# Two-layer attention and expert step on one core: the probabilities and reciprocals turned by pairs of 64-row transposes instead of whole 128-row ones

## The chip, the cores and the metric

The kernel runs on one core of one Trainium2 chip. The metric is the device time of one execution in microseconds; of several executions the median counts.

## The reference, cut to what matters

One inference step of a two-layer model with D = 1024 and 16 heads, all in float32. The 640 tokens are 512 latent tokens and 128 context tokens. Layer 0 mixes tokens by latent attention (MLA), layer 1 by neighbourhood attention (NAT); each is followed by a mixture of 16 experts.

```python
# layer 0, for each head: 64 + 32 columns of q and k, 64 of v
s = einsum('bqhd,bkhd->bhqk', q_blk, k).astype(float32) * MLA_SCALE
p = softmax(s, axis=-1)
o = einsum('bhqk,bkhd->bqhd', p, v)          # context tokens read 128 keys, latent tokens 640
x = x + gate * (o.reshape(B, S, 1024) @ w_o)
# layer 1, for each head: a clamped window of local keys with a bias, and the 128 cached keys
p = softmax(concat([s_loc * NAT_SCALE + bias, s_ctx * NAT_SCALE]), axis=-1)
o = einsum('brnqhd,brankhd->brnqhd', p_loc, vg) + einsum('bhrnqc,bchd->brnqhd', p_ctx, v_ctx)
```

## The kernel before

The kernel is written with semaphores by hand: each engine (PE = TensorE, ACT = ScalarE, DVE = VectorE, POOL, SP) has its own instruction list, and waits on counts that others raise. The order on each engine is therefore fixed in the program. PSUM is one tensor `PS` of 8 banks with 512 float32 columns each.

Both attentions run 40 units of work `w` (`NW`), in eight pairs of heads (`p`), with five query tiles of 128 tokens for each pair (`i`); `ORDER` puts the context tile first (`i == 0`), then the four latent tiles. Inside a unit `par` is 0 or 1 for the two heads of the pair. A unit passes through these steps, each one iteration of the loop later than the one before where the stages allow it:

- Scores on PE (`mla_scores`, lines 979 and 980 for latent tiles, 982 for the context tile; `nat_scores`, lines 1242, 1247 and 1249). MLA has 640 key columns for each head, in banks 0 and 1 for the first head and 2 and 3 for the second; the context tile has 128. NAT has 384 or 128.
- Row maximum on DVE (line 1844 in MLA, 2199 and 2203 in NAT), then the exponential on ACT (line 1481), which also sums each row. The exponentials P lie in `Pm` (MLA) or `Pn` (NAT), tokens on the partitions.
- P is turned, so that keys lie on the partitions, by PE transposes of 128x128 blocks against an identity (line 723, called by `mla_pT` and `nat_pT`). They go to banks 4 and 5, and in MLA the fifth block of each head to bank 6. ACT copies the first head's blocks out (`pT_out`, line 1489) and DVE the second head's (line 1821), in MLA 512 and 768 columns, in NAT 384 and 384.
- The values product on PE (`mla_pv`, line 1010; `nat_pv`, line 1275), 64 output partitions for each head, into bank 7.
- The division by the row sums: DVE takes the reciprocals of the two sums (`rinv`, line 1813), and PE spreads them over a tile of 64 partitions for each head by two float32 products with the identity (`rinv_rows`, line 1020), into bank 6. ACT copies the values product out of PSUM (`o_out`, line 1496), and DVE multiplies it by the spread rows (`o_out` of DVE, a multiply on line 1621).

In MLA, iteration `w` of PE first waits until both copies (`pT_out`) of unit w-2 are through (`a_pa`, `a_pd`). Then it may turn q for a coming head (`q_head`, also line 723; at i = 0 and i = 3), run a slice of the modulation product (`ada`, line 738; at i = 1), or build keys (`k_heads`, line 938; at i = 2). Then it runs the scores of w, the reciprocal rows of w-2, the transposes of w-1 and the values product of w-2. At i = 0 the reciprocal rows also wait for ACT's copy of the turned q (`q_out`, line 1411). ACT's order in an iteration is `q_out` or `k_half` if any, exponentials of w (two), `pT_out` of w-1, `o_out` of w-2. DVE's order is maxima of w (two), `pT_out` of w-1, `o_out` of w-2, `rinv` of w.

In NAT, iteration `w` of PE runs scores of w, transposes of w-2, reciprocal rows and values product of w-3. ACT runs the exponentials of w, `pT_out` of w-2, `o_out` of w-3. DVE runs maxima of w, `rinv` of w-1 (which waits for the values product of w-3), `pT_out` of w-2, `o_out` of w-3 (which waits for ACT's `o_out`).

Of the kernel before, what the change touches and what calls it, by code (L numbers as in the profile page):

```python
# [29 lines left out]
P = 128  # L30
# [86 lines left out]
def build(nc, a, o):  # L117

    with ExitStack() as ctx:
# [45 lines left out]

        def big(off, n, k=None):
            assert off + n <= 20480
            v = BIG[:, off:off + n]
            return v if k is None else v.rearrange("p (k n) -> p k n", k=k)
# [129 lines left out]
        RB = 6 * 512 + 256  # L299
# [417 lines left out]
        def _(pe):  # L717
# [246 lines left out]
            def mla_scores(w):  # L964
# [6 lines left out]
                for par in range(2):  # L971
# [12 lines left out]

            def mla_pT(w):

                if w >= 1:
                    pe.wait_ge(a_pa, w)
                    pe.wait_ge(a_pd, w)
                blocks = NT if w % NT else 1  # L990
                for par in range(2):
                    pe.wait_ge(a_ex, 2 * w + par + 1)
                    for c in range(blocks):
                        dst = bank(4 + par, P, c * P) if c < 4 else bank(6, P, par * P)
                        ins = transpose(dst, Pm[w % 2][par][:, c * P:(c + 1) * P])
                    ins.then_inc(a_pt, 1)

            def mla_pv(w):
# [5 lines left out]
                cols = slice(t * P, (t + 1) * P) if i else slice(0, P)  # L1004
                blocks = [(c, c) for c in range(NT)] if i else [(0, 5)]
                for c, kt in blocks:
                    for par in range(2):
                        h = 2 * p + par
                        at = 1024 + par * P if c == 4 else par * 512 + c * P
                        ins = pe.matmul(PS[64 * par:64 * par + 64, 7 * 512 + cols.start:7 * 512 + cols.stop],  # L1010
# [3 lines left out]

            def rinv_rows(l, w):

                at = 108 + 2 * (w % 2)
                pe.wait_ge(a_ri, NW * l + w + 1)
                for par in range(2):
                    pe.matmul(PS[64 * par:64 * par + 64, RB:RB + P], st[:, at + par:at + par + 1].to_broadcast([P, 64]), ident,  # L1020
                              start=True, stop=True)

            for w in range(NW + 2):
# [28 lines left out]
                if w >= 2:  # L1052
                    pe.wait_ge(a_pd, w - 1)
                    pe.wait_ge(a_o, w - 2)
                    rinv_rows(0, w - 2)
                if 1 <= w <= NW:
                    mla_pT(w - 1)
                if w >= 2:
                    mla_pv(w - 2)
# [192 lines left out]
            def nat_pT(w):  # L1252
# [3 lines left out]
                for par in range(2):  # L1256
                    pe.wait_ge(a_ex, 2 * NW + 2 * w + par + 1)
                    for c in range(3 if w % NT else 1):
                        ins = transpose(bank(4 + par, P, c * P), Pn[w % 3][par][:, c * P:(c + 1) * P])
                    ins.then_inc(a_pt, 1)  # L1260

            def nat_pv(w):
# [4 lines left out]
                pe.wait_ge(a_o, NW + w)  # L1267
                rinv_rows(1, w)
                cols = slice(t * P, (t + 1) * P) if i else slice(0, P)
                vals = [[nv[:, 0], nv[:, 1], nvc], [nvs[:, 0], nvs[:, 1], nvc], [nvs[:, 1], nvs[:, 2], nvc],  # L1270
                        [nv[:, 2], nv[:, 3], nvc], [nv[:, 4]]][t]
                for c, v in enumerate(vals):
                    for par in range(2):
                        h = 2 * p + par
                        ins = pe.matmul(PS[64 * par:64 * par + 64, 7 * 512 + cols.start:7 * 512 + cols.stop],
# [10 lines left out]
            for w in range(NW + 3):  # L1286
# [6 lines left out]
                if w >= 3:  # L1293
                    nat_pv(w - 3)
# [5 lines left out]
        def _(act):  # L1300
# [182 lines left out]
            def pT_out(l, w, dst, n):  # L1483

                g = NW * l + w
                act.wait_ge(a_pt, 2 * g + 1)
                if w >= 2:
                    act.wait_ge(a_pv, g - 1)
                act.activation(dst[:, 0:n], bank(4, n), ACT.Copy).then_inc(a_pa, 1)

            def o_out(l, w):
# [4 lines left out]
                act.activation(OT[:, p, t * P:(t + 1) * P], bank(7, P, t * P if i else 0), ACT.Copy).then_inc(a_oc, 1)  # L1496
# [4 lines left out]
            for w in range(NW + 2):  # L1501
# [14 lines left out]
                if 1 <= w <= NW:  # L1516
                    pT_out(0, w - 1, PTm[(w - 1) % 2], 512 if (w - 1) % NT else P)
# [73 lines left out]
            for w in range(NW + 3):  # L1591
# [10 lines left out]
                if 2 <= w < NW + 2:  # L1602
                    pT_out(1, w - 2, PTn[w % 2][0], 384 if (w - 2) % NT else P)
# [8 lines left out]
        def _(dve):  # L1612
# [193 lines left out]
            def rinv(l, w):  # L1806
# [6 lines left out]
                dve.reciprocal(st[:, 108 + at:110 + at], st[:, 104 + at:106 + at]).then_inc(a_ri, 1)  # L1813
# [9 lines left out]
            def o_out(l, w):  # L1823
# [5 lines left out]
                tt(ot, ot, PS[:, RB:RB + P], ALU.mult).then_inc(a_o, 1)  # L1829

            for w in range(NW + 2):
# [13 lines left out]
                if 1 <= w <= NW:  # L1845
                    n = 768 if (w - 1) % NT else P
                    pT_out(0, w - 1, PTm[(w - 1) % 2][:, 512:512 + n], PS[:, 5 * 512:5 * 512 + n])
# [333 lines left out]
            for w in range(NW + 3):  # L2181
# [24 lines left out]
                if 2 <= w < NW + 2:  # L2206
                    n = 384 if (w - 2) % NT else P
                    pT_out(1, w - 2, PTn[w % 2][1][:, 0:n], bank(5, n))
# [65 lines left out]
```

## Time and profile before

| what | value |
|---|---|
| median of 3 runs | 1399.61 us (1393.13 to 1405.5) |
| profiled execution, span from first to last instruction | 1404.2 us |
| mean granted TensorE clock, share of full | 0.978 |
| MLA attention, 161.0 to 395.5 us of the span | PE busy 220.27 of 234.50 us |
| NAT attention, 968.5 to 1072.0 us of the span | PE busy 95.37 of 103.50 us |
| whole span | PE 91%, DVE 40%, ACT 24%, POOL 17% |

The span is one profiled execution; it lies inside the range of the three runs. A PE instruction's duration runs from its start to the modelled end of its results, so instructions that follow each other overlap in the record, and PE can be called busy in a stretch in which its array is not full. "PEld" is the loading of the stationary operand.

### The profile page before, as it was taken

How to read it: one execution, taken by the hardware profiler on the slowest of the kernel's cores; microseconds unless marked ns; L12 is line 12 of the kernel's file. 1: busy time of each engine (PE TensorE's matmuls, PEld its weight loads, DVE VectorE, ACT ScalarE, POOL GpSimd, SP SyncE). 2: the span in 40 equal slices, each digit the busy share in tenths (PEclk: the TensorE clock that was granted, in tenths of full speed). 3: DMA queues.
4: the chain of work that ended last, by engine and by line, in shares of the span. 5: the costliest groups of instructions: out<-in, count | busy, mean ns of one | idle time of the engine just before them, and what ended most of it. 6: DMA issues, size and time to landing. Idle time of an engine off the chain costs nothing.

```text
span 1404.2 us, 19127 instructions
## 1 busy us (share of the span) xinstructions
PE 1283.3 (91%) x7399; PEld 740.6 (53%) x7399; DVE 568.4 (40%) x1454; ACT 339.7 (24%) x823; POOL 232.8 (17%) x298
## 2 busy tenths in 40 slices
PE   5999899999999989998949999999998998999991
PEld 3665466666654554444424455656775446445440
DVE  5122344444535664444322000002664576444443
ACT  3121344444422310000012000003664231000102
POOL 7122300010010012123221100013221001211231
PEclk8999999999999999999979999999999999999996
DMA  9413211122464459999583363145122615999966
GB/s 388 148 39 153 87 62 62 62 105 78 179 247 164 152 193 390 381 380 395 118 249 125 121 225 120 61 173 165 50 66 95 242 62 225 391 379 380 337 171 210
DMA packets 45449, 267.82 MB, mean 191 GB/s; under 512 B 6980, under 2 KB 13460, under 8 KB 31520
## 3 DMA queue, kind: packets, MB, share of 16 engines
q1 hardware_dynamic: 22672, 192.85, 35.1%
q0 software_dynamic: 16928, 52.77, 13.8%
q10 hardware_dynamic: 5760, 20.97, 3.8%
q8 instruction: 60, 0.98, 0.3%
q14 instruction: 29, 0.24, 0.0%
HBM read 230.19 MB, written 34.81 MB: 189 GB/s over the span
## 4 chain that ended last, share of the span: by engine, by line
PE 70%; DMA 14%; DVE 6%; issue 5%; ACT 4%; DVEq 0%; ACTq 0%; POOLq 0%; SPq 0%
PE PS L851 12%; DMA xrows<-big,info 10%; PE PS L1217 10%; PE PS L1079 10%; PE PS L1127 9%; PE PS L723 8%; PE PS L1144 4%; PE PS L979 4%; PE PS L738 3%; DMA xrows<-big 3%; PE PS L1010 2%; PE PS L938 2%; PE PS L1020 2%; DVE big L1621 1%; ACT weights L1481 1%
## 5 line engine op out<-in xcount | busy, mean ns | idle before, releaser
L1079 PE MATMUL PS<-weights,ht 128*128 128x512 f32 x320 | 142.3, 596 | 2.3 <-DVE ht L1621 1.6
L1217 PE MATMUL PS<-ht,weights 128*128 128x128 f32 (+1 forms) x512 | 140.2, 434 | 1.5 <-PE PS L738 0.9
L723 PE MATMUL PS<-const,big 128*128 128x128 f32 (+2 forms) x611 | 90.1, 284 | 37.8 <-DVE big L2151 17.8
L851 PE MATMUL PS<-weights,ht 128*128 128x336 f32 (+1 forms) x320 | 118.2, 528 | 2.6 <-ACT ht L1399 1.6
L1127 PE MATMUL PS<-big 128*128 128x512 f32 x256 | 115.8, 606 | 4.7 <-DVE big L2068 4.7
L723 PEld LDWEIGHTS PS<-const,big 128*128 128x128 f32 (+2 forms) x611 | 74.1, 144 | 84.1 <-issue 58.2
L1217 PEld LDWEIGHTS PS<-ht,weights 128*128 128x128 f32 x512 | 77.8, 191 | 64.1 <-issue 64.1
L1079 PEld LDWEIGHTS PS<-weights,ht 128*128 128x128 f32 x320 | 59.0, 190 | 69.7 <-issue 69.7
L1530 ACT ACTIVATE big<-PS 128x256 f32<-128x256 f32 x34 | 13.1, 385 | 329.4 <-PE PS L1127 329.4
L851 PEld LDWEIGHTS PS<-weights,ht 128*128 128x128 f32 x320 | 61.0, 193 | 54.5 <-issue 41.1
L1127 PE MATMUL PS<-weights,big 128*128 128x512 f32 x192 | 84.4, 592 | 0.0
L663 POOL DMA_INDIRECT xrows<-big,info x28 | 47.0, 1678 | 221.5 <-DMA xrows<-big,info 213.8
L541 POOL DMA_DIRECT2D modrows<-modrow x32 | 18.7, 586 | 389.0 <-DVE modrow L1621 271.6
L1127 PEld LDWEIGHTS PS<-big 128*128 128x128 f32 x256 | 48.5, 194 | 60.8 <-issue 58.9
L1621 DVE TENSOR_TENSOR big<-PS,big 128x512 f32<-128x512 f32 (+1 forms) x70 | 44.2, 672 | 88.4 <-PE PS L1144 46.7
L1481 ACT ACTIVATE rows<-PS,stats 128x640 f32<-128x640 f32 (+1 forms) x80 | 56.6, 708 | 77.6 <-DVE stats L1844 69.1
L1844 DVE TENSOR_REDUCE stats<-PS 128x1 f32<-128x640 f32 (+1 forms) x80 | 56.8, 718 | 39.6 <-PE PS L980 37.8
L979 PE MATMUL PS<-big 96*128 96x512 f32 x128 | 67.8, 611 | 3.0 <-PE PS L738 1.3
L1144 PE MATMUL PS<-rows,big 128*128 128x512 f32 x144 | 65.0, 594 | 1.0 <-DVE big L2082 1.0
L851 PE MATMUL PS<-weights,rows 128*128 128x384 f32 (+1 forms) x168 | 61.0, 519 | 0.8 <-PE PS L851 0.6
L1621 DVE TENSOR_TENSOR big<-big,PS 128x256 f32<-128x256 f32 x34 | 14.3, 420 | 109.1 <-ACT big L1530 109.1
L1144 PE MATMUL PS<-weights,big 128*128 128x512 f32 x128 | 57.6, 593 | 0.0
(247 smaller groups left out, 1815.3 us busy)
## 6 DMA issues: line engine op xcount, KB each, us to landing
weights<-in_ada SPq DMA_DIRECT2D x22, 2048.0 KB, 8.8
big<-in_gu SPq DMA_DIRECT2D x16, 2048.0 KB, 19.9
weights<-in_gu SPq DMA_DIRECT2D x12, 2048.0 KB, 21.1
rows<-in_down SPq DMA_DIRECT2D x18, 1024.0 KB, 12.4
weights<-in_down SPq DMA_DIRECT2D x16, 1024.0 KB, 16.0
ht<-in_gu SPq DMA_DIRECT2D x6, 2048.0 KB, 22.3
weights<-in_qkv SPq DMA_DIRECT2D x6, 2048.0 KB, 10.2
weights<-in_wo SPq DMA_DIRECT2D x4, 2048.0 KB, 8.6
```

Source lines behind the costliest of these rows:

```text
L663: pool.indirect_dma_start(xD[l], bass.IndirectOffsetOnAxis(ap=token.bitcast(U32), axis=0), yb[par], None, compute_op=ALU.add).then_inc(e_y ...
L723: return pe.transpose(dst, src, const[0:n, C_ID:C_ID + n])
L738: ins = pe.matmul(PS[32 * g:32 * g + 2, ada_out_at(i):ada_out_at(i) + P], condT[:, 2 * k:2 * k + 2], w[:, k, g * P:(g + 1) * P], start=(k ...
L851: ins = pe.matmul(bank(4 + u % 2, n), lhs(k), rhs(k), start=(k == 0), stop=(k == ks - 1))
L979: pe.matmul(bank(2 * par), lhs, kTh[h % 4][0:QD, 0:512], start=True, stop=True)
L1079: ins = pe.matmul(bank(4 + j), OT[:, k, t * P:(t + 1) * P], w[j][:, k, :], start=(k == 0), stop=(k == KD - 1))
L1127: ins = pe.matmul(bank(0), gatT[:, k, :], w[:, k, :], start=(k == 0), stop=(k == KD - 1))
L1144: ins = pe.matmul(bank(out + n), actT[:, k, :], w[:, k, n * 512:(n + 1) * 512], start=(k == 0), stop=(k == 1))
L1217: ins = pe.matmul(bank(bb, n1 - n0), w[:, k, m * P:(m + 1) * P], hT[:, k, n0:n1], start=(k == 0), stop=(k == KD - 1))
L1481: act.activation(dst, src, ACT.Exp, scale=sign, bias=st[:, 100 + at:101 + at], accum_out=st[:, 104 + at:105 + at]).then_inc(a_ex, 1)
L1621: return dve.tensor_tensor(dst, x, y, op)
L1844: dve.tensor_reduce(st[:, at:at + 1], bank(2 * par, n), AXX, ALU.max, negate=True).then_inc(a_mx, 1)
```

## The change

Every 128-row transpose of P becomes two transposes of 64 rows each: the lower 64 partitions of the block against the lower 64 columns of the identity, the upper against the upper. Each half writes 64 columns over all 128 partitions, and the two halves go to two PSUM banks, 512 columns apart. In MLA the first head's blocks take banks 4 and 5 and the second head's banks 6 and 7, at 64 columns for each block; in NAT both heads use banks 4 and 5. The copies put the halves together again: in MLA ACT takes the first head's 640 columns and DVE the second head's 640; in NAT ACT takes bank 4 and DVE bank 5, both heads each, and ACT waits until both heads are turned.

The reciprocal rows are no longer a product: DVE writes each reciprocal into 64 columns of an SBUF tile (`spread_rinv`, 128 columns for a unit), and PE turns this tile with one pair of half transposes into banks 6 and 7 at column 320. In MLA it stands between the two heads' transposes, in NAT behind them.

The values product moves out of bank 7 in MLA, into bank 1 at column 256, a bank that also holds columns 512 to 639 of the first head's scores. So `mla_pv` of w-2 waits for the first exponential of w, and the second score product of the first head waits for `o_out` of w-3. In NAT it stays in bank 7.

```diff
+        spread_rinv = [R[:, 1280:1536], R[:, 4608:4864]]
...
-        RB = 6 * 512 + 256
+        RI = 6 * 512 + 320
+        PV = (512 + 256, 7 * 512)
...
+        def mla_blocks(w, par):
+
+            n = NT if w % NT else 1
+            dst = PTm[w % 2][:, par * 640:par * 640 + n * P].rearrange("p (c r n) -> p c r n", r=2, n=64)
+            src = PS[:, (4 + 2 * par) * 512:(6 + 2 * par) * 512].rearrange("p (r c n) -> p c r n", r=2, n=64)
+            return dst, src[:, 0:n]
+
+        def nat_blocks(w, r):
+
+            n = 3 if w % NT else 1
+            at = 6400 + w % 2 * 768
+            dst = W[:, at:at + 768].rearrange("p (x c r n) -> p x c r n", x=2, r=2, n=64)[:, :, 0:n, r]
+            src = bank(4 + r).rearrange("p (x c n) -> p x c n", x=2, n=64)
+            return dst, src[:, :, 0:n]
...
+            def transpose_halves(dst, src, at):
+
+                for r in range(2):
+                    rows = slice(64 * r, 64 * r + 64)
+                    ins = pe.transpose(dst[:, at + 512 * r:at + 512 * r + 64], src[rows], const[rows, C_ID + 64 * r:C_ID + 64 * r + 64])
+                return ins
...
                     if t < CTX:
                         pe.matmul(bank(2 * par), lhs, kTh[h % 4][0:QD, 0:512], start=True, stop=True)
+                        if par == 0 and w >= 3:
+                            pe.wait_ge(a_oc, w - 2)
...
+            def rinv_rows(l, w):
+
+                at = w % 2 * P
+                pe.wait_ge(a_ri, NW * l + w + 1)
+                pe.wait_ge(a_o, NW * l + w)
+                transpose_halves(PS, spread_rinv[l][:, at:at + P], RI)
+
             def mla_pT(w):
 
-                if w >= 1:
-                    pe.wait_ge(a_pa, w)
-                    pe.wait_ge(a_pd, w)
                 blocks = NT if w % NT else 1
                 for par in range(2):
+                    if w >= 1:
+                        pe.wait_ge((a_pa, a_pd)[par], w)
+                    if par and w >= 1:
+                        rinv_rows(0, w - 1)
                     pe.wait_ge(a_ex, 2 * w + par + 1)
                     for c in range(blocks):
-                        dst = bank(4 + par, P, c * P) if c < 4 else bank(6, P, par * P)
-                        ins = transpose(dst, Pm[w % 2][par][:, c * P:(c + 1) * P])
+                        ins = transpose_halves(PS, Pm[w % 2][par][:, c * P:(c + 1) * P], (4 + 2 * par) * 512 + c * 64)
                     ins.then_inc(a_pt, 1)
 
             def mla_pv(w):
...
-                cols = slice(t * P, (t + 1) * P) if i else slice(0, P)
+                if w + 2 < NW:
+                    pe.wait_ge(a_ex, 2 * (w + 2) + 1)
...
-            def rinv_rows(l, w):
-
-                at = 108 + 2 * (w % 2)
-                pe.wait_ge(a_ri, NW * l + w + 1)
-                for par in range(2):
-                    pe.matmul(PS[64 * par:64 * par + 64, RB:RB + P], st[:, at + par:at + par + 1].to_broadcast([P, 64]), ident,
-                              start=True, stop=True)
...
-                        ins = transpose(bank(4 + par, P, c * P), Pn[w % 3][par][:, c * P:(c + 1) * P])
+                        ins = transpose_halves(PS, Pn[w % 3][par][:, c * P:(c + 1) * P], 4 * 512 + par * 256 + c * 64)
...
-                dve.reciprocal(st[:, 108 + at:110 + at], st[:, 104 + at:106 + at]).then_inc(a_ri, 1)
+                dst = spread_rinv[l][:, w % 2 * P:(w % 2 + 1) * P].rearrange("p (x n) -> p x n", x=2)
+                dve.reciprocal(dst, st[:, 104 + at:106 + at].unsqueeze(2).to_broadcast([P, 2, 64])).then_inc(a_ri, 1)
```

## Rows read from the trace of the kernel before

**Rows 1.** Busy time by stretch: MLA, NAT, and one inside the first experts.

```profile
161.00:395.50 234.50, 220.27 (x2080) 149.22 (x2078) 112.06 (x215) 105.02 (x259) 18.50 (x32) 1.00 0.24 91
968.50:1072.00 103.50, 95.37 (x1034) 74.72 (x1034) 66.31 (x260) 68.45 (x237) 17.00 (x24) 1.00 0.24 68
...
560.00:595.00 35.00, 35.00 (x105) 17.00 (x104) 15.84 (x30) 2.95 (x6) 5.11 (x4) 1.00 1.02 379
```

**Rows 2.** Timeline, MLA, latent tile i = 4: start, duration, engine, line.

```profile
298.94 1.12 PE L979 MATMUL PS<-big 96*128 96x512 f32 x2
...
301.30 0.44 PE L1020 MATMUL PS<-const,stats 128*64 128x128 f32 x4
...
301.67 1.07 PEld L723 LDWEIGHTS PS<-const,rows 128*128 128x128 f32 x10 [0.17 <-issue]
...
301.93 0.19 ACT L1481 ACTIVATION_READ_ACCUMULATOR rows<-PS,stats 128x1 f32 x1
302.32 0.80 ACT L1481 ACTIVATE rows<-PS,stats 128x640 f32<-128x640 f32 x1 [0.20 <-issue]
302.91 1.07 PEld L1010 LDWEIGHTS PS<-rows,big 128*64 128x64 f32 x20 [0.17 <-issue]
...
303.10 0.59 ACT L1489 ACTIVATE route<-PS 128x512 f32<-128x512 f32 x1
304.15 0.50 PEld L723 LDWEIGHTS PS<-const,big 128*96 128x96 f32 x5 [0.17 <-issue]
```

**Rows 3.** Timeline, MLA, the context tile i = 0 that follows.

```profile
305.69 0.44 PE L1020 MATMUL PS<-const,stats 128*64 128x128 f32 x4 [0.34 <-ACT big L1411]
...
308.55 1.64 PEld L738 LDWEIGHTS PS<-weights,condT 128*2 128x2 f32 x64 [0.17 <-issue]
```

**Rows 4.** Timeline, MLA, i = 1 and the start and end of i = 2.

```profile
285.04 0.27 ACT L1489 ACTIVATE rows<-PS 128x128 f32<-128x128 f32 x1
...
285.36 0.20 PEld L938 LDWEIGHTS PS<-rows,weights 128*64 128x64 f32 x4 [0.31 <-ACT rows L1489]
...
288.09 0.30 PEld L979 LDWEIGHTS PS<-big 96*128 96x128 f32 x2 [0.39 <-issue]
...
293.24 0.50 PEld L723 LDWEIGHTS PS<-const,big 128*96 128x96 f32 x5 [0.98 <-ACT route L1489]
```

**Rows 5.** Timeline: four products of 128 columns, whole array, and in two 64-row tiles.

```profile
304.74 0.61 PE L982 MATMUL PS<-big 96*128 96x128 f32 x4
...
1006.74 0.39 PE L1247 MATMUL PS<-big 64*128 64x128 f32 x4
```

**Rows 6.** Groups of instructions by shape: count, busy us, mean ns, idle before.

```profile
L723 PEld LDWEIGHTS PS<-const,rows 128*128 128x128 f32 x338 | 36.3, 140 | 7.0 <-issue 6.9
...
L723 PEld LDWEIGHTS PS<-const,big 128*96 128x96 f32 x80 | 8.1, 126 | 10.1 <-ACT route L1489 3.9 <-issue 3.2 <-ACT rows L1489 3.0
...
L1585 ACT ACTIVATE big<-PS 128x640 f32<-128x640 f32 x8 | 5.6, 704 | 135.1 <-PE PS L1217 135.1
```

**Rows 7.** Timeline, NAT, from i = 4 to the context tile and beyond.

```profile
1012.97 0.62 ACT L1481 ACTIVATE weights<-weights,stats 128x384 f32<-128x384 f32 x1 [0.83 <-DVE stats L2199]
...
1015.64 0.61 ACT L1481 ACTIVATE weights<-weights,stats 128x384 f32<-128x384 f32 x1 [0.83 <-DVE stats L2199]
...
1016.86 0.47 ACT L1489 ACTIVATE weights<-PS 128x384 f32<-128x384 f32 x1
...
1017.55 0.64 PEld L723 LDWEIGHTS PS<-const,weights 128*128 128x128 f32 x6 [0.61 <-ACT weights L1489]
...
1018.10 0.37 ACT L1481 ACTIVATE weights<-PS,stats 128x128 f32<-128x128 f32 x1 [0.61 <-issue]
...
1019.50 0.28 ACT L1496 ACTIVATE ht<-PS 128x128 f32<-128x128 f32 x1 [0.22 <-PE PS L1275]
1019.57 0.17 DVE L1813 RECIPROCAL stats<-stats 128x2 f32<-128x2 f32 x1 [1.36 <-PE PS L1275]
...
1020.94 0.62 ACT L1481 ACTIVATE weights<-weights,stats 128x384 f32<-128x384 f32 x1 [1.16 <-DVE stats L2199]
```

More of the change, by code:

```diff
@@ L1008, in mla_pv @@
                         h = 2 * p + par
-                        at = 1024 + par * P if c == 4 else par * 512 + c * P
-                        ins = pe.matmul(PS[64 * par:64 * par + 64, 7 * 512 + cols.start:7 * 512 + cols.stop],
+                        at = par * 640 + c * P
+                        ins = pe.matmul(PS[64 * par:64 * par + 64, PV[0]:PV[0] + P],
                                         mv[:, kt, h * VD:(h + 1) * VD], PTm[w % 2][:, at:at + P],
@@ L1051, in _ @@
                         pe.wait_ge(q_ea, 2 * p + 4)
[L1052 to L1055, printed above, removed]
                 if 1 <= w <= NW:
@@ L1058, in _ @@
                 if w >= 2:
+                    if w > NW:
+                        pe.wait_ge(a_pd, NW)
+                        rinv_rows(0, w - 2)
                     mla_pv(w - 2)
@@ L1274, in nat_pv @@
                         h = 2 * p + par
-                        ins = pe.matmul(PS[64 * par:64 * par + 64, 7 * 512 + cols.start:7 * 512 + cols.stop],
+                        ins = pe.matmul(PS[64 * par:64 * par + 64, PV[1]:PV[1] + P],
                                         v[:, h * VD:(h + 1) * VD], PTn[w % 2][par][:, c * P:(c + 1) * P],
@@ L1293, in _ @@
                 if w >= 3:
+                    rinv_rows(1, w - 3)
                     nat_pv(w - 3)
@@ L1481, in exp, with pT_out @@
                 act.activation(dst, src, ACT.Exp, scale=sign, bias=st[:, 100 + at:101 + at], accum_out=st[:, 104 + at:105 + at]).then_inc(a_ex, 1)
-            def pT_out(l, w, dst, n):
+            def pT_out(l, w, dst, src):
                 g = NW * l + w
-                act.wait_ge(a_pt, 2 * g + 1)
+                act.wait_ge(a_pt, 2 * g + 1 + l)
                 if w >= 2:
                     act.wait_ge(a_pv, g - 1)
-                act.activation(dst[:, 0:n], bank(4, n), ACT.Copy).then_inc(a_pa, 1)
+                act.activation(dst, src, ACT.Copy).then_inc(a_pa, 1)
             def o_out(l, w):
@@ L1495, in o_out @@
                 act.wait_ge(a_pv, NW * l + w + 1)
-                act.activation(OT[:, p, t * P:(t + 1) * P], bank(7, P, t * P if i else 0), ACT.Copy).then_inc(a_oc, 1)
+                act.activation(OT[:, p, t * P:(t + 1) * P], PS[:, PV[l]:PV[l] + P], ACT.Copy).then_inc(a_oc, 1)
             warm(ACT.Exp)
@@ L1516, in _ @@
                 if 1 <= w <= NW:
-                    pT_out(0, w - 1, PTm[(w - 1) % 2], 512 if (w - 1) % NT else P)
+                    pT_out(0, w - 1, *mla_blocks(w - 1, 0))
                 if w >= 2:
@@ L1602, in _ @@
                 if 2 <= w < NW + 2:
-                    pT_out(1, w - 2, PTn[w % 2][0], 384 if (w - 2) % NT else P)
+                    pT_out(1, w - 2, *nat_blocks(w - 2, 0))
                 if w >= 3:
@@ L1828, in o_out @@
                 ot = OT[:, p, t * P:(t + 1) * P]
-                tt(ot, ot, PS[:, RB:RB + P], ALU.mult).then_inc(a_o, 1)
+                rows = PS[:, 6 * 512:8 * 512].rearrange("p (r n) -> p r n", r=2)[:, :, RI - 6 * 512:RI - 6 * 512 + 64]
+                ot = ot.rearrange("p (r n) -> p r n", r=2)
+                tt(ot, ot, rows, ALU.mult).then_inc(a_o, 1)
             for w in range(NW + 2):
@@ L1845, in _ @@
                 if 1 <= w <= NW:
-                    n = 768 if (w - 1) % NT else P
-                    pT_out(0, w - 1, PTm[(w - 1) % 2][:, 512:512 + n], PS[:, 5 * 512:5 * 512 + n])
+                    pT_out(0, w - 1, *mla_blocks(w - 1, 1))
                 if w >= 2:
@@ L2206, in _ @@
                 if 2 <= w < NW + 2:
-                    n = 384 if (w - 2) % NT else P
-                    pT_out(1, w - 2, PTn[w % 2][1][:, 0:n], bank(5, n))
+                    pT_out(1, w - 2, *nat_blocks(w - 2, 1))
                 if w >= 3:
```

3 lines of the change are left out of this document (removed).

## The prediction

> **What bounds the kernel now.** I read the windows first. The change touches only the two attentions, 338 us of the span, and in both PE is busy for over nine tenths of the time [rows 1]. That invites the sum "PE work saved = time saved". The granted clock is 1.00 there, so nothing of the time is a low clock. Then I read the timeline of one full latent tile, to see whether each engine is really waited for. From 298.94 to 304.15 PE runs scores, reciprocal rows, transposes, values product, with no wait but short ones marked "issue" of 0.17 us in front of each new kind of array tile [rows 2]. So this tile, 5.21 us long, is bound by PE. But ACT is close behind: its second exponential starts at 302.32, its copy of the turned block at 303.10 and ends at 303.69, and PE may not begin the next tile before that copy is through. It is only 0.46 us ahead of PE. That chain is what I follow below: scores, maximum, exponentials, copy, next scores. At i = 1 it already ends last: PE waits 0.31 us for ACT's copy [rows 4]. In NAT the same shape of loop runs over ACT and DVE, and most tiles there already go at its pace; the clearest places where PE ends last are around the context tile [rows 7].
>
> **The price of transposes and of a mode change.** Ten transposes and what follows them until the next instruction of another kind take 302.91 - 301.67 = 1.24 us. The reciprocal rows (two pairs of column tiles of 128 columns) and their change take 301.67 - 301.30 = 0.37 us [rows 2]. The difference of 0.87 us is eight steps: 0.109 us for one step of 128 columns, and 0.37 - 0.22 = 0.15 us for one change of array tiling.
>
> **The price of a pair of half transposes.** The trace has no transposes in row tiles, so it is bounded. From above, at full price and unoverlapped: two halves at 0.109 us each, 0.22 us. From below: half the columns of a full step, both halves at once, 0.055 us. The nearest row is the NAT scores: four products of 128 columns in two row tiles take 0.39 us against 0.61 us for four in the whole array [rows 5]. With about 0.27 us for the last to complete, that is one step instead of three, so row tiles do overlap in pairs. The load side: a transpose's stationary load takes 140 ns for 128 columns and 126 ns for 96 [rows 6], 0.44 ns a column, so 56 ns for 128; two overlapping loads keep up with 55 ns of streaming. I take 0.057 us a pair.
>
> The Trainium skill, "TensorE: Matmul & The Clock Gate", section "LDWEIGHTS (loading the stationary operand)", speaks against this: a load costs its columns over 1.2 GHz whatever its rows, some 107 ns for 128 columns, and halving the rows saves none of it. By that a pair would cost as much as a whole transpose (an estimate from that page), and the time would come out as in rival B. The trace's slope over columns (56 ns for 128) does not agree for transposes.
>
> **MLA, tile by tile.** On PE a full tile drops ten steps to ten pairs (10 x 0.052 = 0.52 us), and the reciprocal rows from 0.22 us plus a change of 0.15 us to one pair, 0.057 us (0.31 us less; the rows now share the transposes' mode, so three changes remain of four). That is 0.83 us off PE. How much of it is time depends on the chain behind ACT:
>
> - i = 3 and i = 4. The second exponential starts 302.32 - 298.94 = 3.38 us after the scores start. Nothing of the change touches it. The copy can start 0.78 us later (303.10, [rows 2]), and now has 640 columns instead of 512: 0.70 us by a copy of that size [rows 6], not 0.59. With 0.05 us to PE the next tile starts 3.38 + 0.78 + 0.70 + 0.05 = 4.91 us after this one, against 5.21: 0.30 us gained, not 0.83. The new wait of the values product on the first exponential (its sum read ends at 301.93 + 0.19 = 302.12, [rows 2]) lets it start at 302.17 at best; PE would get there at 301.30 + 11 x 0.057 + 0.15 = 302.08. It costs 0.1 us and is hidden, because the product then ends near 303.5, before ACT's copy (303.80). Queued behind it on PE are the next scores, which wait for that copy anyway.
> - i = 2. The same chain: 293.24 - 288.09 = 5.15 us from scores to the next q transposes [rows 4] becomes 4.91: 0.24 us.
> - i = 1. Already set by ACT, whose copy is small and stays as it is: nothing gained. The new wait delays the values product by some 0.1 us, which fits in the 0.31 us idle in front of line 938 [rows 4].
> - i = 0. The exponentials are short, so PE sets the end. From 305.69, where ACT's copy of q releases it, to 308.55 is 2.86 us [rows 3], and the full 0.83 us goes. DVE's copy of the second head ends by about 307.4 (305.69, 0.63 us of pairs, 0.25 to their end, and 0.82 for 640 columns, an estimate from ACT's rate), and PE is ready at 307.7.
>
> The wait of the first head's second score product for `o_out` is free: ACT's `o_out` follows the copy that releases PE, and is through 0.3 us later; the product is issued 0.5 us after the scores start. The wider reciprocal adds some 0.1 us on DVE (128 columns instead of 2), in front of maxima that come over 0.4 us later.
>
> Sum for MLA: i = 2 to 4, eight times, 8 x (0.24 + 0.30 + 0.30) = 6.7; i = 0, seven times with a full tile behind it, 5.8; the tail 0.6. Together 13.1 us.
>
> **NAT.** On PE a full tile drops 6 x 0.052 + 0.16 + 0.15 = 0.62 us. Scores and half transposes are both in 64-row tiles, so there too one change goes. But the loop of ACT and DVE (exponentials, copy, `o_out` of ACT, `o_out` of DVE, maximum, next exponential) takes 1015.64 - 1012.97 = 2.67 us without waiting for PE [rows 7], and the next one, to 1018.10, 2.46 us. These stay. From the context tile's exponential (1018.10) to the next (1020.94) is 2.84 us, since ACT's and DVE's steps wait for the values product (0.22 and 1.36 us idle, [rows 7]). That product follows transposes that start at 1017.55, 0.22 us after ACT's copy ended at 1016.86 + 0.47. Without a mode change they start at 1017.4; 7 pairs take 0.40 us, the change 0.15, the product 0.65, its completion 0.17: done near 1018.8 instead of 1019.5. DVE then gives back 0.1 us with its wider reciprocal. I count 0.59 us, seven times, and 0.07 us in one more tile of each pair: 4.7 us.
>
> **Sum.** 13.1 + 4.7 = 17.8 us off the profiled 1404.2 us, 1386.4. Taken off the median of the runs (the profiled execution lies 4.6 us above it), 1399.6 - 17.8 = 1381.8 us. Nothing later should take it back: in the expert stage PE is busy for 35.00 us of 35 [rows 1], its weight loads are released by PE and by the end of attention, and so shift with it. DMA's share is 1.02 there, so were loads the limit the saving could be lost; a PE without idle time speaks against that.
>
> **Rivals.** A change of under 1%, 14 us, can hardly be told from none here, so the cases are sorted by that bound.
>
> - A. The chain behind ACT does not bind, and PE's saving is all time. In MLA 31 full tiles x 0.83 + the tail's share + 8 small ones x 0.42 make 30 us; in NAT (4 x 0.62 + 0.41) x 8 = 23 us. That gives 1347 us. PE's share of nine tenths speaks for it; against it stand the explicit waits, with 0.46 us of slack. Chance 0.07.
> - B. A pair costs a whole step, 0.109 us. PE then saves 0.31 us less a fresh pair's excess in each MLA tile, 0.26 us. At i = 3 and 4 that nearly equals what the chain allows; at i = 0 it loses 0.57 us. MLA gives 8.2 us, NAT about 2.3: 1389 us, within 1%. For it: no row shows a transpose of 64 columns, and a floor for each load or product could lie anywhere up to the whole step. Against: the slope of the loads [rows 6]. Chance 0.14.
> - C. The change does not do what it says: the two halves do not overlap, and each costs a whole step, 0.22 us a pair. At i = 3 and 4 PE needs 11 x 0.218 + 0.15 = 2.55 us where it now needs 1.61: 0.95 us more; i = 0 the same; i = 2, where the small product follows, 0.65. That is 28 us in MLA, and in NAT, where a full tile has 7 x 0.218 + 0.15 = 1.68 us instead of 6 x 0.109 + 0.15 + 0.37 = 1.17, 2.1 us more for each pair of heads less some 0.7 us of idle PE, 11 us: 1399.6 + 39 = 1438 us, slower. It decides from 0.133 us a pair, where 11 pairs and a change take the present 1.61 us. Against it stands the 0.39 us of [rows 5]. Chance 0.08.
> - D. Half-filled tiles lower the granted clock in NAT. At its lower level, 1.2 instead of 2.4 GHz, PE's stream alone would add tens of us. Nothing in the trace shows it: the present 64-row scores run at 1.00. Chance 0.02.
>
> **How the numbers follow.** My forecast, 1382 us, has 0.66; what none of the cases names, 0.03, I put at no change. Nearly all of the forecast's chance lies beyond 14 us: 0.63, and 0.07 of A, make 0.70 faster. B, 0.03 of the forecast and the rest make 0.20 the same. C and D make 0.10 slower. The range leaves out A, C and D and a little of the edges. Its low end, 1369, lets the chain be 0.1 us shorter in a tile and adds the scatter of the runs (6 us); its high end, 1393, takes in B and 4 us of scatter.
>
> **What the changed profile would show.** A row of ten half-transpose pairs (20 records) lasts about 0.8 us, not 1.31. Two `issue` stops in a MLA tile fall behind the transposes and behind the values product, none between reciprocal rows and transposes. A latent tile takes 4.9 us, and PE's wait in front of line 979 and 723 names ACT's copy (line 1489), 0.3 to 0.5 us each. The copy's duration is 0.70 us. The stretch from ACT's q copy to `ada` at i = 0 shrinks from 2.86 to 2.03 us. NAT shrinks from 103.5 to 99 us. I would be wrong if the copy, with its two-bank pattern, took much over 0.7 us, if the pairs ran at 0.11 us or more, or if the values product's wait for the exponential reached ACT's chain.

## The result and the profile after

The changed kernel takes 1407.98 us (median of 12 runs, 1400.54 to 1412.29) beside 1400.7 us before (median of 12, one of which took 1957.95 us): ratio 1.0047, 95% interval 1.003 to 1.0064. It is half a per cent slower, where 1.3% faster was forecast. The profiled execution has a span of 1410.5 us. The twelve executions of the changed kernel fall into two groups, five of 1400.5 to 1403.8 us with a mean granted clock of 0.974 or 0.975 and seven of 1407.7 to 1412.3 us with 0.966 to 0.970, and the profiled one is the slowest of all.

The two attentions moved in opposite directions. From its first to its last scores MLA takes 215.7 us instead of 225.4. NAT takes 112.5 us instead of 97.8, and what follows NAT's last scores 343.5 instead of 338.0. The windows of the changed kernel, for the stretches of [rows 1] that hold the attentions (NAT now starts some 14 us earlier, 9.7 us of it through MLA, so the second is not the same work):

```profile
161.00:395.50 234.50, 207.52 (x2358) 138.34 (x2359) 140.05 (x219) 108.12 (x262) 21.93 (x39) 0.99 0.29 108
968.50:1072.00 103.50, 77.54 (x1038) 61.15 (x1034) 82.07 (x229) 59.12 (x205) 16.28 (x24) 0.95 0.16 41
```

Columns as in [rows 1]: DVE's busy time (the third) has grown from 112 to 140 us and from 66 to 82 us, although the change gave it hardly any new instruction; the clock (third from the right) is no longer 1.00.

MLA first. The timeline of the latent tile i = 4 (from 293.18, behind i = 3) and the context tile, loads of PE and the steps of ACT, to be held against [rows 2] and [rows 3]:

```profile
293.18 0.30 PEld L1004 LDWEIGHTS PS<-big 96*128 96x128 f32 x2 [0.51 <-ACT rows L1513]
...
295.54 0.77 PEld L747 LDWEIGHTS PS<-const,rows 64*128 64x128 f32 x22
...
296.47 1.10 PEld L1045 LDWEIGHTS PS<-rows,big 128*64 128x64 f32 x20 [0.17 <-issue]
...
296.56 0.80 ACT L1505 ACTIVATE rows<-PS,stats 128x640 f32<-128x640 f32 x1 [0.20 <-PE PS L747]
...
297.34 0.69 ACT L1513 ACTIVATE route<-PS 128x640 f32<-128x640 f32 x1
...
298.09 0.50 PEld L741 LDWEIGHTS PS<-const,big 128*96 128x96 f32 x5 [0.51 <-ACT route L1513]
...
299.63 0.90 PE L747 MATMUL PS<-const,rows 64*128 64x64 f32 x22 [0.34 <-ACT big L1435]
...
300.46 1.31 PE L1045 MATMUL PS<-route,big 128*64 128x128 f32 x20
...
301.70 1.64 PEld L763 LDWEIGHTS PS<-weights,condT 128*2 128x2 f32 x64 [0.17 <-issue]
```

A latent tile lasts 298.09 - 293.18 = 4.91 us, and PE stands 0.51 us in front of the next, released by ACT's copy (line 1513, once 1489). Eleven pairs of half transposes, the reciprocal's among them, and one mode change take 300.46 - 299.63 = 0.83 us: 0.062 us a pair with a change of 0.15 us. There is no `issue` stop left between reciprocal rows and transposes.

In NAT the lines of DVE explain the tile. From the start of one context tile's scores to the next:

```profile
1010.15 0.30 PEld L1275 LDWEIGHTS PS<-big 64*128 64x128 f32 x4 [0.17 <-issue]
...
1013.37 0.95 DVE L1838 RECIPROCAL rows<-stats 128x128 f32<-128x128 f32 x1 [1.09 <-PE PS L1298]
...
1014.24 0.49 DVE L1846 COPY weights<-PS 128x384 f32<-128x384 f32 x1
1014.66 0.27 DVE L1645 TENSOR_TENSOR ht<-ht,PS 128x128 f32<-128x128 f32 x1
1014.81 0.48 PEld L747 LDWEIGHTS PS<-const,weights 64*128 64x128 f32 x12 [0.89 <-issue]
...
1014.84 0.55 DVE L2225 CUSTOM_DVE_ANT_1 weights<-PS,rows 128x384 f32<-128x384 f32 x1
...
1015.44 0.62 ACT L1505 ACTIVATE weights<-weights,stats 128x384 f32<-128x384 f32 x1 [1.86 <-DVE stats L2225]
...
1024.50 0.30 PEld L1275 LDWEIGHTS PS<-big 64*128 64x128 f32 x4 [0.17 <-issue]
```

A pair of heads takes 14.35 us; before, with the same marks, 13.07 us. DVE waits 1.09 us for the values product (line 1298), only then starts a reciprocal of 0.95 us, and behind it stand its copy, `o_out` and the next maximum; the exponential of the first latent tile waits 1.86 us for that maximum (line 2225), where the same one waited 1.16 us before ([rows 7], 1020.94). PE stands 0.89 us in front of the transposes. The row says only `issue`; by the code PE waits for both copies there, and DVE's ends at 1014.24 + 0.49 = 1014.73, ACT's long before. In [rows 7] the same reciprocal took 0.17 us. The group of all 80:

```profile
L1838 DVE RECIPROCAL rows<-stats 128x128 f32<-128x128 f32 x80 | 76.0, 949 | 28.2 <-PE PS L1298 25.7 <-ACT rows L1505 1.4 <-ACT weights L1505 0.5
```

And the granted clock, which was 1.00 throughout both attentions before. Windows in NAT (two pairs of heads at full clock, then two stretches at half) and in the output projection behind it:

```profile
1010.15:1024.50 14.35, 10.54 (x152) 8.35 (x150) 11.78 (x33) 8.49 (x31) 2.82 (x4) 1.00 0.22 58
1038.90:1053.20 14.30, 10.49 (x153) 8.31 (x152) 11.78 (x33) 8.52 (x31) 2.83 (x4) 1.00 0.21 57
961.80:972.60 10.80, 9.43 (x90) 7.62 (x90) 6.05 (x19) 5.00 (x18) 2.82 (x4) 0.53 0.29 75
1054.50:1061.30 6.80, 6.45 (x60) 5.18 (x60) 3.37 (x11) 3.14 (x11) 0.00 (x0) 0.51 0.00 0
1071.60:1085.20 13.60, 10.44 (x69) 6.66 (x66) 2.96 (x7) 3.30 (x7) 3.06 (x6) 0.50 0.26 73
```

In this execution TensorE runs at 1.2 instead of 2.4 GHz for some 31 us. Another such stretch, 3.4 us at 167 us, falls into the first heads of MLA.

### The profile page after: what moved, and what is told of

Its sections match the earlier page's. It is cut to its first block, busy times and chain, and to the rows that moved or that the text cites. A ratio compares the mean times of both kernels' runs of the same rounds, so it can differ in the third digit from the quotient of the medians.

```text
span 1410.5 us, 19920 instructions
## 1 busy us (share of the span) xinstructions
PE 1254.7 (89%) x7783; PEld 723.2 (51%) x7783; DVE 620.8 (44%) x1454; ACT 341.0 (24%) x823; POOL 234.5 (17%) x298
## 4 chain that ended last, share of the span: by engine, by line
PE 49%; DMA 14%; DVE 4%; issue 4%; ACT 2%; ACTq 0%; DVEq 0%; POOLq 0%
DMA xrows<-big,info 10%; PE PS L1243 10%; PE PS L1105 10%; PE PS L1153 9%; PE PS L876 5%; PE PS L1170 4%; DMA xrows<-big 3%; PE PS L741 2%; PE PS L1298 2%; PE PS L747 2%; PE PS L763 1%; DVE big L1645 1%; PE PS L1268 1%; DMA resid<-xrows 1%; ACT big L1336 1%
## 5 line engine op out<-in xcount | busy, mean ns | idle before, releaser
L1838 DVE RECIPROCAL rows<-stats 128x128 f32<-128x128 f32 x80 | 76.0, 949 | 28.2 <-PE PS L1298 25.7
L1153 PE MATMUL PS<-weights,big 128*128 128x512 f32 x192 | 84.4, 592 | 0.0
L1645 DVE TENSOR_TENSOR big<-big,PS 128x256 f32<-128x256 f32 x34 | 14.3, 420 | 101.0 <-ACT big L1554 101.0
```

Source lines behind the costliest of these rows:

```text
L1153: ins = pe.matmul(bank(0), gatT[:, k, :], w[:, k, :], start=(k == 0), stop=(k == KD - 1))
L1645: return dve.tensor_tensor(dst, x, y, op)
L1838: dve.reciprocal(dst, st[:, 104 + at:106 + at].unsqueeze(2).to_broadcast([P, 2, 64])).then_inc(a_ri, 1)
```

## The experiments

The theories were: W, the reciprocal of 128 columns eats the gain, as it lies in DVE's loop in NAT; D, the thinner PE stream lowers the clock, and that alone costs the gain; L, the copies' two-bank layout is dearer. Theory A is the forecast's own (and the opposite of the prediction's rival A): MLA's tile is set by the chain behind ACT. "Pair of heads" is the time from one pair's context tile to the next pair's in the trace, at full clock. The kernel before, run beside each group, took 1400.8, 1400.9 and 1401.5 us. The medians are of 12 executions for the change, of 10 for after_pad, copy_pad, whole_copy and before4, and of 4 for the others; each trace is one execution.

| kernel | us (median) | ratio, 95% interval | MLA pair | NAT pair |
|---|---|---|---|---|
| before | 1400.7 | | 29.74 | 13.07 |
| the change | 1407.98 | 1.003 to 1.0064 | 28.10 | 14.35 |
| narrow_copy | 1390.46 | 0.9907 to 0.994 | 28.10 | 12.91 |
| before_wide | 1424.21 | 1.0154 to 1.0188 | 29.74 | 16.12 |
| mla_only | 1389.56 | 0.9902 to 0.9943 | 28.10 | 13.07 |
| after_pad | 1404.16 | 1.002 to 1.0043 | 28.11 | 14.50 |
| after4 | 1382.64 | 0.9863 to 0.993 | 28.11 | 12.69 |
| copy_pad | 1398.05 | 0.9957 to 0.9994 | 28.11 | 13.74 |
| mla_early | 1383.95 | 0.9873 to 0.9926 | 27.77 | 13.07 |
| whole_copy | 1397.12 | 0.9962 to 0.9989 | 28.62 | 13.45 |
| before4 | 1398.12 | 0.9967 to 0.9999 | 29.74 | 12.94 |
| best_wide | 1383.25 | 0.9859 to 0.9931 | 27.77 | 12.69 |
| best_copy | 1386.78 | 0.988 to 0.9943 | 27.77 | 12.69 |

**narrow_copy**: the reciprocal of two columns, spread by a copy.

```diff
-                dve.reciprocal(dst, st[:, 104 + at:106 + at].unsqueeze(2).to_broadcast([P, 2, 64])).then_inc(a_ri, 1)
+                link(dve.reciprocal(st[:, 108 + at:110 + at], st[:, 104 + at:106 + at]))
+                dve.tensor_copy(dst, st[:, 108 + at:110 + at].unsqueeze(2).to_broadcast([P, 2, 64])).then_inc(a_ri, 1)
```

> The changed kernel, but DVE takes the reciprocal of the two sums only (0.16 us) and spreads it by a copy of 128 columns (about 0.3 us) in place of one reciprocal of 128 columns (0.95 us). Theory W (the wide reciprocal eats the gain: it lies in DVE's loop in NAT): NAT's 14.35 us for a pair of heads falls to about 12.6 us, the total to about 1384 us, 1.2% below the kernel before, and the stretches of half clock in and behind NAT go, because PE waits less. Theory D (the thinner PE stream by itself lowers the clock and costs the gain): the stretches stay and the time stays above 1394 us. Theory L (the two-bank layout of the copies is dearer): the time stays within 3 us of the changed kernel's 1408 us.

1390.46 us, 17.5 us less than the change. W holds for the most part, 6 us short of its figure, with the stretches of half clock that D expected. L is out: the layout is untouched, and ACT's copy of 384 columns takes 0.47 us in both layouts ([rows 7], and after4's row below). The two instructions and the copy behind them:

```profile
1002.53 0.17 DVE L1838 RECIPROCAL stats<-stats 128x2 f32<-128x2 f32 x1 [0.39 <-PE PS L1298]
1002.74 0.23 DVE L1839 COPY rows<-stats 128x128 f32<-128x128 f32 x1
...
1002.88 0.55 DVE L1847 COPY weights<-PS 128x384 f32<-128x384 f32 x1
```

The spreading of 128 columns itself costs 0.23 us; it is the reciprocal that is dear by the column. From the start of the reciprocal to the copy behind it pass 0.35 us, against 0.87 us in the change and 0.10 us before. NAT's pair of 12.91 us is 0.3 us over the expectation, and the clock still falls: 3.4 us in NAT, 10.2 us behind it. So not all of the low clock went with the wide reciprocal.

**before_wide**: the kernel before, with the wide reciprocal.

```diff
-                dve.reciprocal(st[:, 108 + at:110 + at], st[:, 104 + at:106 + at]).then_inc(a_ri, 1)
+                dst = spread_rinv[l][:, w % 2 * P:(w % 2 + 1) * P].rearrange("p (x n) -> p x n", x=2)
+                dve.reciprocal(dst, st[:, 104 + at:106 + at].unsqueeze(2).to_broadcast([P, 2, 64])).then_inc(a_ri, 1)
...
-                    pe.matmul(PS[64 * par:64 * par + 64, RB:RB + P], st[:, at + par:at + par + 1].to_broadcast([P, 64]), ident,
+                    pe.matmul(PS[64 * par:64 * par + 64, RB:RB + P], spread_rinv[l][:, at + 64 * par:at + 64 * par + 64], ident,
```

> The kernel before with one edit: the reciprocal is taken over 128 columns and the products read these columns. Theory W: MLA stays within 2 us (DVE has slack there), NAT gains about 0.8 to 1.2 us for each pair of heads: 1408 to 1412 us in all without a drop of the clock, up to 1420 with one. Theories D and L: the reciprocal is hidden, 1400 to 1402 us.

1424.21 us, 23 us slower: twice what W said. A pair of heads of NAT grows by 3.05 us, which is 0.61 us for each of the five tiles, about three quarters of the added 0.79 us. MLA does not move at all. That is W in its cleanest form. The rest of the change, put on this kernel, brings NAT from 16.12 to 14.35 us. The clock stays at 1.00 in NAT, although PE waits more than before:

```profile
958.10:1078.40 120.30, 91.12 (x984) 71.34 (x986) 87.28 (x249) 64.94 (x226) 16.95 (x24) 1.00 0.20 58
```

**mla_only**: MLA as changed, wide reciprocal included; transposes, copies, products and narrow reciprocals of NAT as before.

```diff
             def rinv_rows(l, w):
...
+                if l:
+                    at = 108 + 2 * (w % 2)
+                    for par in range(2):
+                        pe.matmul(PS[64 * par:64 * par + 64, RB:RB + P], st[:, at + par:at + par + 1].to_broadcast([P, 64]), ident,
+                                  start=True, stop=True)
+                    return
...
-                        ins = transpose_halves(PS, Pn[w % 3][par][:, c * P:(c + 1) * P], 4 * 512 + par * 256 + c * 64)
+                        ins = transpose(bank(4 + par, P, c * P), Pn[w % 3][par][:, c * P:(c + 1) * P])
```

> MLA as in the changed kernel, wide reciprocal and all; NAT as in the kernel before. Theory W: MLA keeps its 10 to 13 us, NAT loses nothing: 1388 to 1391 us. Theory L: MLA's part is no gain either: 1398 to 1403 us. Theory D: the clock drops in MLA too and takes back over 3 us: above 1393 us.

1389.56 us: MLA's part of the change is a gain of 11 us, and its wide reciprocal is free there. That is with a stretch of half clock of 3.4 us in its first pair of heads, at 162 us.

**after_pad**: the change, with filler for PE in NAT.

```diff
-                    for par in range(2):
+                    for par in (0, 1, 0, 1):
                         pe.matmul(bank(at + par, LOCAL), qT[half[par], p, t * P:(t + 1) * P], kT[half[par], p, KEY0[t]:KEY0[t] + LOCAL],
...
-                for par in range(2):
+                for n, par in enumerate((0, 1, 0, 1)):
...
-                    ins.then_inc(a_s, 1)
+                    if n >= 2:
+                        ins.then_inc(a_s, 1)
```

> The changed kernel with each score product of NAT run twice into the same place, some 0.65 us more PE work in a latent tile, where PE now waits 0.7 to 0.9 us: the result is the same, only PE is denser. Theory D and the part of W that goes through the clock: the half-clock stretches at 962 to 973, 1054 to 1061 and 1072 to 1085 us vanish, NAT's pair of heads stays near 14.3 us, the total falls by 5 to 9 us to 1399 to 1403 us. If the clock has another cause the stretches stay and the total is 1408 to 1412 us.

1404.16 us, 3.8 us less with more work in it, and 1 us over the range expected. The half-clock stretches in NAT are gone, the one behind it stays:

```profile
954.70:1064.00 109.30, 99.59 (x1388) 83.53 (x1390) 88.39 (x249) 64.52 (x226) 16.87 (x24) 1.00 0.22 64
...
1068.40:1082.10 13.70, 10.54 (x66) 6.63 (x64) 2.96 (x7) 3.30 (x7) 3.19 (x7) 0.51 0.26 74
```

Without filler the second whole pair of heads took 16.38 us, with it 14.49 us. Its ten executions have mean clocks of 0.973 to 0.978, those of the change 0.966 to 0.975. This points to a clock in NAT that hangs on how dense PE is, and that had its own price there. It is not shown beyond that: the stretches differ between executions of one kernel, and each trace is one of them.

**after4**: the change, with four buffers for the spread reciprocals.

```diff
-        spread_rinv = [R[:, 1280:1536], R[:, 4608:4864]]
+        spread_rinv = [R[:, 1280:1792], R[:, 4608:5120]]
...
-                if w >= 2:
-                    dve.wait_ge(a_pv, g - 1)
+                if w >= 4:
+                    dve.wait_ge(a_pv, g - 3)
```

> The changed kernel with four buffers for the spread reciprocals instead of two, so that the reciprocal of unit w-1 need not wait for the values product of w-3. It stays 0.95 us long. Theory W in its sharp form (the reciprocal costs because it starts only when the product is done, and the copies and the next maximum queue behind it): it now runs while DVE waited 0.4 to 1.1 us for the product, NAT's pair of heads falls from 14.35 to about 13.2 us, the total to about 1396 us. If its length on DVE alone counted (DVE full), it stays at 14.3 us and 1406 us.

1382.64 us, 25 us less than the change by this alone, and much better than expected. The reciprocal is as long as ever, and nothing waits for it:

```profile
1008.22 0.95 DVE L1838 RECIPROCAL rows<-stats 128x128 f32<-128x128 f32 x1
...
1009.07 0.47 ACT L1513 ACTIVATE weights<-PS 128x384 f32<-128x384 f32 x1
1009.08 0.49 DVE L1846 COPY weights<-PS 128x384 f32<-128x384 f32 x1
...
1009.73 0.29 DVE L1645 TENSOR_TENSOR ht<-ht,PS 128x128 f32<-128x128 f32 x1 [0.16 <-ACT ht L1520]
```

It starts right behind the maximum, in the time in which DVE used to wait for the values product, and its copy starts together with ACT's. A pair of heads takes 12.69 us, less than before the change. No stretch of half clock is left in either attention or in the output projection. The exponential of the first latent tile waits 1.08 us for the maximum, instead of 1.86 in the change and 1.16 before it:

```profile
1012.74 0.62 ACT L1505 ACTIVATE weights<-weights,stats 128x384 f32<-128x384 f32 x1 [1.08 <-DVE stats L2225]
```

So the length of the reciprocal and DVE's load cost nothing by themselves; they cost through the place that the wait gives the reciprocal. Shortening it in that place (narrow_copy) gave back 17.5 of these 25 us.

**copy_pad**: narrow_copy with the filler of after_pad.

> The kernel with narrow reciprocal and copy (1390.5 us), with each NAT score product run twice, as filler for PE. Theory D: its half-clock stretches at 989 us (3.4 us long) and behind NAT at 1058 us (10.2 us) vanish, the stretch behind the last scores of NAT falls from 341.4 to about 338 us; a tile of NAT gains at most 0.1 us: 1386 to 1390 us. If the filler costs more than the clock gives, it shows as a longer pair of heads than 12.91 us: 1391 to 1395 us.

1398.05 us, over both ranges: the expectation failed. Here the filler is in the way, a pair of heads goes from 12.91 to 13.74 us, and the stretch of half clock behind NAT (10.2 us long at 1064 us) stays. The one in NAT (989 us) is gone, as with after_pad.

**mla_early**: mla_only, and PE no longer waits for both copies at i = 1 and i = 4.

```diff
-                    if w >= 2:
+                    if w >= 2 and i not in (1, 4):
                         pe.wait_ge(a_pa, w - 1)
                         pe.wait_ge(a_pd, w - 1)
-                    else:
+                    if w < 2:
                         pe.wait_ge(q_ea, 2)
```

> MLA changed, NAT as before (1389.6 us), and in MLA PE no longer waits for both copies in front of the scores of i = 1 and i = 4, where it writes nothing to banks 4 to 7 before them. Theory A (the chain exponential, copy, wait, next scores sets MLA's tile): the scores of i = 4 start 0.5 us earlier, the pair of heads falls from 28.10 to about 27.6 us, the total by 4 us to 1385.5 us. If another chain binds, it stays at 28.1 us and 1389.5 us.

1383.95 us, 5.6 us less than mla_only. PE's loads at i = 4:

```profile
286.88 0.30 PEld L1003 LDWEIGHTS PS<-big 96*128 96x128 f32 x2 [0.17 <-issue]
...
290.28 1.10 PEld L1050 LDWEIGHTS PS<-rows,big 128*64 128x64 f32 x20 [0.27 <-issue]
...
291.79 0.50 PEld L740 LDWEIGHTS PS<-const,big 128*96 128x96 f32 x5 [0.41 <-ACT route L1518]
```

The 0.51 us in front of the scores is gone; of it, 0.34 us reach the pair of heads (28.10 to 27.77): the values product now stands 0.27 us instead of the 0.17 us of a mode change, and in front of i = 0 PE still waits 0.41 us for ACT's copy. Eight pairs make 2.7 of the 5.6 us. Some 1.7 us more is the first pair, in which the stretch of half clock of mla_only's trace is missing here. Theory A holds.

**whole_copy**: narrow_copy with whole transposes. Each copy then reads one bank, and the values product and the reciprocal rows change places between banks 6 and 7.

```diff
-                        ins = transpose_halves(PS, Pm[w % 2][par][:, c * P:(c + 1) * P], (4 + 2 * par) * 512 + c * 64)
+                        ins = transpose(bank(4 + 2 * par, P, c * P), Pm[w % 2][par][:, c * P:(c + 1) * P])
...
-                transpose_halves(PS, spread_rinv[l][:, at:at + P], RI)
+                transpose(PS[:, RI:RI + P], spread_rinv[l][:, at:at + P])
```

> As narrow reciprocal and copy, but every pair of half transposes is again one whole transpose of 128 rows, the reciprocal's too; layout and waits otherwise as in the change. It prices the halves. By the chain behind ACT (theory A): i = 2 to 4 of MLA stay near 4.91 us, since a whole step more for each block is hidden behind ACT but for some 0.05 us; at i = 0, where PE sets the end, 11 steps cost 0.109 instead of 0.062 us, 0.5 us more, less nothing for modes: the pair of heads rises from 28.10 to 28.6 to 28.8 us. NAT 12.91 us rises to about 13.1 us. Total 1395 to 1397 us. If the halves bought nothing, 1390 us; if PE's work counted in full everywhere, 1405 us.

1397.12 us, 6.7 us more than with halves: 0.52 us for a pair of heads in MLA, where only the tile i = 0 could pay, and 0.54 us in NAT. Eleven whole transposes and the start of the values product in MLA's context tile:

```profile
299.42 1.42 PE L737 MATMUL PS<-const,rows 128*128 128x128 f32 x11 [0.34 <-ACT big L1431]
300.76 1.31 PE L1041 MATMUL PS<-route,big 128*64 128x128 f32 x20
```

From the start of these transposes to that of the products it is 1.34 us, against 0.83 us for eleven pairs of halves: 0.51 us, MLA's whole difference.

**before4**: the kernel before, with four pairs of reciprocals and the same freed wait as after4.

```diff
-                if w >= 2:
-                    dve.wait_ge(a_pv, g - 1)
+                if w >= 4:
+                    dve.wait_ge(a_pv, g - 3)
                 at = 2 * (w % 2)
-                dve.reciprocal(st[:, 108 + at:110 + at], st[:, 104 + at:106 + at]).then_inc(a_ri, 1)
+                to = 2 * (w % 4)
+                dve.reciprocal(st[:, 108 + to:110 + to], st[:, 104 + at:106 + at]).then_inc(a_ri, 1)
```

> The kernel before with four pairs of reciprocals in place of two, so that the reciprocal of w-1 need not wait for the values product of w-3; no transposes changed. It tells whether after4's gain in NAT (13.07 to 12.69 us for a pair of heads) is the freed wait alone. If it is: 12.6 to 12.8 us here too, 1397 to 1398 us. If PE's transposes still hold the context tile up, as the prediction had it: 12.9 to 13.07 us, 1399 to 1401 us.

12.94 us for NAT's pair of heads, as expected for the case that the transposes still hold the context tile up: a third of after4's 0.38 us is the freed wait alone, 0.25 us the rest of the change, its transposes above all. The total, 1398.12 us, is barely below before (0.9967 to 0.9999) and does not decide between the two cases.

**best_wide** (after4 with mla_early's wait) and **best_copy** (the same with the narrow reciprocal and a copy).

> The changed kernel with four buffers for the spread reciprocals and, in MLA, no wait for the copies in front of the scores of i = 1 and 4. If both are independent: MLA 27.77 us and NAT 12.69 us for a pair of heads, 1382.6 - 2.8 = about 1380 us.

> As best_wide, with the narrow reciprocal and a copy (0.16 + 0.23 us) in place of the reciprocal of 128 columns (0.95 us). If the wide reciprocal is fully hidden once it need not wait, this is the same within 1 us (about 1380 us, NAT 12.69 us); if its length still costs, NAT falls to 12.5 us and the total to 1378 us.

1383.25 and 1386.78 us. In the traces both parts add up, 27.77 and 12.69 us in both kernels, so the wide reciprocal is hidden in full once it need not wait. The totals do not show the further 2.8 us over after4 (1382.64 us): the intervals overlap, and best_copy's execution has another stretch of half clock (3.4 us at 1020 us) which best_wide's, with the same pair of heads, has not. after4 and best_wide are 1.0% faster than the kernel before and 1.8% faster than the change.

## Why the prediction was wrong

By its own steps:

- **What bounds MLA: right.** A latent tile was to take 4.91 us and takes 4.91; i = 2 4.91 (measured: 4.91); i = 1 unchanged; i = 0 2.03 us from ACT's release to `ada` (2.07). The pair of heads was to fall by 1.67 us and falls by 1.64. mla_only and mla_early show the mechanism. From first to last scores MLA falls by 9.7 us; the sum had 13.1 us for the whole stage. The first pair of heads lost 1.7 us to half clock, and the last tile and the tail behind it lie outside the 9.7.
- **The pair of half transposes: right**, 0.062 us instead of 0.057, so rivals B and C fall; rival A falls by PE's wait of 0.51 us for ACT's copy. The copy of 640 columns takes 0.69 us as forecast. The figure for loads that the prediction cites from the Trainium skill, "TensorE: Matmul & The Clock Gate", section "LDWEIGHTS (loading the stationary operand)", is not borne out for transposes: two loads of 128 columns and their products take 0.062 us together here.
- **The step that failed: "The wider reciprocal adds some 0.1 us on DVE (128 columns instead of 2)".** It adds 0.79 us: 0.949 us against 0.162. I had taken a column's price from copies. The trace of before held reciprocals of 1 and 2 columns only, both 162 ns long, so its own rows could not show the slope, and I neither bounded the price from above nor asked what it would cost if it were large. It got no rival, and none of the three signs of being wrong that the prediction names came up. A bound at both ends was needed; the point at which it decides was near, since in NAT I had named the loop of ACT and DVE as the bound. The Trainium skill, "VectorE: DVE Perf Modes", section "First, the fixed hardware budget", does say that the reciprocal runs through an iterative divide with a repeat count of 8. No run here shows the count. The changed kernel's rows (6.2 ns a column between 2 and 128, where a copy of 128 columns takes 227 ns in all) agree with it in that a column is dear, and the sentence would have called for a rival.
- **What followed from it.** `rinv` waits for the values product of w-3, and I had read that wait in the code and in [rows 7]. In MLA the added time is free (before_wide: 29.74 us unchanged). In NAT it stands between the product and what follows on DVE, the copy, `o_out` and the maximum that the next exponential waits for: 14.35 instead of 12.69 us (after4) for a pair of heads, about 13 us in all.
- **Rival D, at 0.02, came true in part and in another place.** The clock falls to 1.2 GHz for 31 us in and behind NAT in the profiled execution. What hangs on it there: 2 us in the second whole pair of heads (16.38 against 14.39 in the next), 5.5 us behind NAT's last scores (343.5 against 338.0), 1.7 us in the first pair of MLA (25.92 against 24.27 in after4's, from its first scores), and a part of the last pair; some 10 us. The 1.7 us are no mark of the half transposes: before4, with whole ones, has the same stretch (26.81 against 25.13 us in the kernel before). With the 13 us above this is 23 of the 29.8 us between the spans of the two profiled executions (1410.5 and 1380.7 us); 2.5 us more had passed before MLA began, and the rest is not assigned. The medians are 25 us apart. The reciprocal's 13 us by themselves outweigh the 11 us that MLA gains (mla_only). I had argued from the clock of the present 64-row scores only, not from how much emptier PE would become.
- **NAT's own gain: the mechanism right, the size off.** 0.66 us for a pair of heads was forecast; with the wait freed it is 0.38 us, of which the change gives 0.25 (before4). Between before and narrow_copy it is 0.16 us; there the reciprocal and its copy delay DVE by 0.25 us instead of the 0.1 us that I allowed, which is the likely reason, not tested by itself.
- How near the rest of the forecast was: narrow_copy, whose delay on DVE comes nearest to what I had assumed, takes 1390.5 us, inside the range of 1369 to 1393 and 8.7 us above the forecast. That after4 takes 1382.6 us beside the forecast 1381.8 is luck, as it also frees a wait that the change keeps, and its NAT gains less than I had said.

## What to carry to other kernels

An instruction that a change merely widens is a new instruction: price it by a row of the same operation at the new width, and where there is none, write down the width's worst case and see whose turn comes next in that engine's queue. A short step that waits for a late event and has long steps queued behind it belongs in front of the wait; two more buffers did here what shortening the step did only in part. And where a change makes one engine idle beside another's loop, look at the clock of that engine as well as at its work, and at more than one execution.

## What the runs showed of the hardware

- DVE's reciprocal costs by the column: 162 ns for 2 columns, 949 ns for 128, where a copy of 128 columns takes 227 ns.
- Fp32 transposes in two 64-row tiles overlap: eleven pairs of 64 columns with a mode change take 0.83 us, eleven whole ones with the same change 1.34 us.
- The granted clock did not follow PE's share alone. before_wide keeps 1.00 through NAT with PE busy for 91 of 120 us. In the change, pairs of heads with PE busy for 10.54 and 10.49 us out of some 14.3 run at 1.00, and the last pair, right behind one of them, falls to half clock. best_wide and best_copy have the same pair of heads, and only one of them has a stretch of half clock there. The stretch in the output projection behind NAT came in the change, narrow_copy and both kernels with filler, and in no other run's trace. The one in the first pair of MLA came in the change, narrow_copy, mla_only, both kernels with filler, best_copy and before4, so with whole and with half transposes. What decides either stays open.
